# Score products of two sub-heads issued in turn, for a whole tile at once

## The chip, the cores and the metric

One NeuronCore of a Trainium2 chip runs the whole kernel. The metric is the device time of one execution in microseconds (us). Before the change the median of three runs is 1964.11 us (1963.23 to 1964.5).

## What is computed

The program is one layer of a streaming encoder for two groups of tokens, 1024 prompt tokens and 64 sample tokens, that share all weights: a modulated norm, two token mixers side by side (HGRN2 with 4 heads of 128 key channels, GLA with 4 heads of 64 key channels), a gated merge and an output projection, then a routed mixture of 32 experts and a final norm. All data is fp32. The change lies in the GLA mixer, of which this is the core, for chunks of 64 tokens:

```python
b = cumsum(log_a)                                   # per key channel
o_inter = (q * exp(b)) @ S
diff = b[t] - b[s]
decay = exp(where(causal, diff, 0)) * causal
scores[t, s] = sum_k q[t, k] * k[s, k] * decay[t, s, k]
o = o_inter + scores @ v
S = exp(b_last) * S + (k * exp(b_last - b)).T @ v
```

The decay depends on the key channel, so the scores are no single matrix product. The kernel splits the causal triangle of a chunk into levels of halves (64, 32, ..., 1 tokens). For each level the decay splits into a factor of the key's token and one of the query's token, so that a level is one product of two prepared arrays, of which a mask keeps the blocks that belong to this level.

## The kernel before

The kernel is a row of stages; in each, every engine has its own instruction list, written out by hand, and waits on semaphores. There is no planner. The stage `mixers` runs over six units: two GLA units of two heads each (sub-heads, 64 key channels each, on the lower and the upper 64 partitions), then four HGRN2 units of one head with 128 channels. `SUB[u]` is 2 or 1. A unit projects its inputs for all tokens (matmuls of 360 or 364 tokens, lines 128 to 130), prepares the levels, and then runs a loop over tiles: eight of 128 tokens and one of 64. A step `j` of the loop is one sub-head of one tile, `i, sub = divmod(j, SUB[u])`; a GLA unit has 18 steps.

In a step TensorE does, in this order:

- `turn` (lines 528, 530), at the last sub-head of a tile: transposes the keys and values of the next tile into `p_tok`.
- `scores(u, j + 1)` (lines 544, 547): for each of 7 levels and each half of 64 tokens one product of 64 by 64, from the partitions of the sub-head, into `p_sc[:, j % 2]`, and for a tile of 128 tokens one more product for the cross block (keys of the first half, queries of the second). An fp32 matmul is two instructions. Token half 0 writes output partitions 0 to 63, half 1 writes 64 to 127; each `p_sc[:, x]` is 512 fp32 columns wide, a bank of its own. Before it, `scores(u, j)` waits until all masks up to `j - 2` are through (`sc_masked`) and the cross copies up to there (`cross_ready`).
- the filling: projections of the next unit or gates still to be made (`filled(u, j)`). In a GLA unit nine column blocks are spread over 18 steps, one in each even step.
- `outputs(u, j)` (lines 568 to 570): the old state with the queries, the scores `sc[:, j % 2]` with the values, and the update of the state into `p_u`.

VectorE does in step `j`: `mask(u, j + 1)`, then `advance(u, j)` (line 1010, the state, only at the last sub-head of a tile, after both `outputs`), then other work of the step: the low half of the next weights (`next_low`, line 1022, the step after a filling with a new block), `gate_g` at step 3, `gate_g_scale` at 5, `decay_log` (line 899) three steps and `decay_bound` four steps after the next unit's first block is filled (steps 7 and 8), `gate_x` of the third gate at 13. Within `mask` (lines 990, 995, 997) the order is:

```python
dve.wait_ge(sc_done, after(J0[u] + j + 1))
V.tensor_tensor(diag[...j % 2], p_sc[...j % 2, 0:NL * 64], masks, ALU.mult)   # sc_masked
dve.wait_ge(o_done, after(J0[u] + j - 1))          # outputs up to j - 2 done
V.tensor_copy(sc[0:64, j % 2, 64:P], p_sc[...])    # cross_ready
V.tensor_reduce(...)  # one per half of 64 tokens, sc_ready
```

ScalarE keeps the outputs (`keep_output`), the turned tiles (`keep_tok`, line 747), the projections (`keep`) and computes the exponentials of gates and decays.

Of the kernel before, what the change touches and what calls it, by code (L numbers as in the profile page):

```python
# [34 lines left out]
P = 128  # L35
# [5 lines left out]
NT = T_PROMPT // P  # L41
TILES = [(i * P, P) for i in range(NT)] + [(T_PROMPT, T_SAMPLE)]
# [10 lines left out]
NL = len(HALVES)  # L53
# [3 lines left out]
def after(n):  # L57

    return n + START
# [311 lines left out]
def mixers(nc, a, h_hi, h_lo, ident, mix_d, gate_d, outs, consts):  # L371
# [5 lines left out]
    SUB = [2 if kind == "gla" else 1 for kind, _ in UNITS]  # L377
    NS = [(NT + 1) * n for n in SUB]
# [36 lines left out]
    def filled(u, j):  # L415

        groups = filling(u)
        now = groups[-(-len(groups) * j // NS[u]):-(-len(groups) * (j + 1) // NS[u])]
        return [g for some in now for g in some]
# [14 lines left out]
    with Stage(nc, "x") as s:  # L434
# [69 lines left out]
        @block.tensor  # L504
        def _(pe):
            def project(u, name, c):

                c0, n = COLS[c]
                e = place[(u, name), c]
                pe.wait_ge(proj_kept, after(e - 1))  # L510
                if name == "logit":
                    i = UNITS[u][1]
                    nc.tensor.matmul(p_proj[:, e % 2, 0:n], gk2[:, i * P:(i + 1) * P], lr[:, c0:c0 + n],
                                     start=True, stop=True).then_inc(proj_done, 1)
                    return
                i = load_no[u, name]
                if c == 0:
                    pe.wait_ge(w_lo_done, after(i + 1))
                for k_ in range(KD):
                    m = split_matmul(nc, p_proj[:, e % 2, 0:n], (w_hi[:, i % 2, k_, :], w_lo[:, i % 2, k_, :]),  # L520
                                     (h_hi[:, k_, c0:c0 + n], h_lo[:, k_, c0:c0 + n]), k_ == 0, k_ == KD - 1)
                m.then_inc(proj_done, 1)

            def turn(u, i):

                t0, n = TILES[i]
                pe.wait_ge(tok_kept, after(u * (NT + 1) + i))
                nc.tensor.transpose(p_tok[0:n, 0:P], ke[:, t0:t0 + n], ident[:, :])
                for sub in range(SUB[u]):
                    m = nc.tensor.transpose(p_tok[0:n, (1 + sub) * P:(2 + sub) * P], v[sub][:, t0:t0 + n], ident[:, :])  # L530
                m.then_inc(tok_turned, 1)

            def scores(u, j):

                i, sub = divmod(j, SUB[u])
                t0, n = TILES[i]
                ch = slice(sub * (P // SUB[u]), (sub + 1) * (P // SUB[u]))
                pe.wait_ge(sc_masked, after(J0[u] + j - 1))
                pe.wait_ge(cross_ready, after(X0[u] + min(j, NT * SUB[u]) - 1))
                for l in range(NL):  # L540
                    for h0 in range(0, n, 64):
                        tt = slice(t0 + h0, t0 + h0 + 64)
                        left, right = (k[u % 2], q) if l == 0 else (lev[:, l], lev[:, l])
                        m = nc.tensor.matmul(p_sc[h0:h0 + 64, j % 2, l * 64:(l + 1) * 64], left[ch, tt], right[ch, tt],
                                             start=True, stop=True)
                if n == P:
                    m = nc.tensor.matmul(p_sc[0:64, j % 2, NL * 64:NL * 64 + 64], lev[ch, 0, t0:t0 + 64],  # L547
                                         lev[ch, 0, t0 + 64:t0 + P], start=True, stop=True)
                m.then_inc(sc_done, 1)

            def outputs(u, j):

                i, sub = divmod(j, SUB[u])
                t0, n = TILES[i]
                ch = slice(sub * (P // SUB[u]), (sub + 1) * (P // SUB[u]))
                po = p_o[:, j % 2, 0:n]
                vt = tok[:, i % 2, 1 + sub, :]
                if sub == 0:
                    pe.wait_ge(tok_kept, after(u * (NT + 1) + i + 1))
                    if i == 0:  # L560
                        pe.wait_ge(state_zero, after(u + 1))
                    if i == NT:
                        pe.wait_ge(state_in, landed(u + 1))
                    pe.wait_ge(state_ready, after(u * (NT + 1) + i))
                pe.wait_ge(o_kept, after(J0[u] + j - 1))
                pe.wait_ge(sc_ready, after(J0[u] + j + 1))
                pe.wait_ge(cross_ready, after(X0[u] + min(j + 1, NT * SUB[u])))
                nc.tensor.matmul(po, state[ch, i % 2 if i < NT else 2, :], qe[ch, t0:t0 + n], start=True, stop=False)
                nc.tensor.matmul(po, vt[:, :], sc[:, j % 2, 0:n], start=False, stop=True).then_inc(o_done, 1)
                nc.tensor.matmul(p_u[ch, 0:DV], tok[0:n, i % 2, 0, ch], vt[0:n, :], start=True, stop=True).then_inc(u_done, 1)  # L570

            def mean_square(u, sub, c):

                c0, n = COLS[c]
                pe.wait_ge(o_sq, after(H0[u] + sub + 1))
                pe.wait_ge(rstd_ln, after((H0[u] + sub) * NC + c))
                nc.tensor.matmul(p_tok[:, 0:n], mean[:, :], t1[:, c0:c0 + n], start=True, stop=True).then_inc(ms_done, 1)

            pe.wait_ge(lr_split, after(2))
            for c, (c0, n) in enumerate(COLS):  # L580
                if c:
                    pe.wait_ge(lr_kept, after(c))
                for k_ in range(KD):
                    m = split_matmul(nc, p_tok[0:RANK, 0:n], (lr_hi[:, k_, :], lr_lo[:, k_, :]),
                                     (h_hi[:, k_, c0:c0 + n], h_lo[:, k_, c0:c0 + n]), k_ == 0, k_ == KD - 1)
                m.then_inc(lr_done, 1)
            pe.wait_ge(lr_kept, after(NC))
            for name in first(0):
                for c in range(NC):
                    project(0, name, c)  # L590
            for u in range(NU):
                for n_, name in enumerate(middle(u)):
                    for c in range(NC):
                        project(u, name, c)
                        if u and n_ == 0 and c > 0:
                            mean_square(u - 1, 0, c - 1)
                        if u and n_ == 1 and c == 0:
                            mean_square(u - 1, 0, 2)
                        if u and n_ == 2 and SUB[u - 1] == 2:
                            mean_square(u - 1, 1, c)  # L600
                pe.wait_ge(lev_ready, after((u + 1) * NL))
                pe.wait_ge(ends_ready, after(2 * u + 2))
                pe.wait_ge(proj_kept, kept(u, f"v{SUB[u] - 1}"))
                pe.wait_ge(rstd_ln, after(H0[u] * NC))
                turn(u, 0)
                scores(u, 0)
                for j in range(NS[u]):
                    if j + 1 < NS[u]:
                        if (j + 1) % SUB[u] == 0:
                            turn(u, (j + 1) // SUB[u])  # L610
                        scores(u, j + 1)
                    for (of, name), c in filled(u, j):
                        project(of, name, c)
                    outputs(u, j)
            for c in range(NC):
                mean_square(NU - 1, 0, c)

        @block.scalar
        def _(act):
# [167 lines left out]
            for u in range(NU):  # L787
# [72 lines left out]
                for j in range(NS[u]):  # L860
                    if j:
                        keep_output(u, j - 1)
                    if j + 1 < NS[u] and (j + 1) % SUB[u] == 0:
                        keep_tok(u, (j + 1) // SUB[u])
                    for (of, name), c in filled(u, j):
                        keep(of, name, c)
                    if j < 3:
                        gate_g_part(u, SUB[u] - 1, j)
                    if j == 4:
                        gate_g_exp(u, SUB[u] - 1)  # L870
                    if u + 1 < NU and 0 <= j - filled_by(u, first(u + 1)[0]) < 3:
                        decay_part(u + 1, j - filled_by(u, first(u + 1)[0]))
                    if not HG[u]:
                        if 0 <= j - filled_by(u, "x2") < 3:
                            gate_x_part(u, 2, j - filled_by(u, "x2"))
                        if j == filled_by(u, "x2") + 4:
                            gate_x_out(u, 2)
# [1350 lines left out]
```

## Time and profile before

| | |
|---|---|
| median of 3 runs | 1964.11 us |
| the profiled execution | 1957.79 us |
| its span, first to last instruction | 1955.9 us |
| mean granted TensorE clock | 0.915 |
| TensorE busy | 1624.9 us (83%) |
| VectorE busy | 1285.5 us (66%) |
| ScalarE busy | 956.5 us (49%) |
| score products, line 544 (PE), GLA tiles | 816 + 136 instructions, 218 to 271 ns each |

### The profile page before, as it was taken

The page shows a single profiled execution, that of the slowest core. Times are in us where ns is not written, and L with a number is a line of the kernel's source. Part 1 is how long each engine was busy: PE and PEld are TensorE (multiplying, and loading weights), DVE is VectorE, ACT ScalarE, POOL GpSimd, SP SyncE. Part 2 cuts the span into 40 slices and gives each one's busy share as a digit, 9 for nine tenths or more (in the row PEclk, how much of TensorE's full clock was granted, in tenths as well). Part 3 has the DMA queues.
Part 4 walks back from the last instruction along what each step waited for, and adds up shares of the span by engine and source line. Part 5 has one row for each costly group of instructions (what it writes and reads, how often), then busy time and mean ns, then how long its engine had stood idle before and what let it go on. Part 6 is the DMA issues. An engine that isn't in the chain of part 4 may idle for free. (4 is left out here: it accounts for less than half of the span.)

```text
span 1955.9 us, 26699 instructions
## 1 busy us (share of the span) xinstructions
PE 1624.9 (83%) x10674; PEld 1414.9 (72%) x10674; DVE 1285.5 (66%) x1623; ACT 956.5 (49%) x1182; POOL 322.2 (16%) x187
## 2 busy tenths in 40 slices
PE   3679999999798999983896995089999999999810
PEld 2459989988698998983895774078888888888710
DVE  2534368267658585854554656189999999999727
ACT  2624335333525353533102211178888888888713
POOL 0110001000101010101220000512232233233113
PEclk8789999999999999996898897589999999999955
DMA  8822102201111111104325322689999999999546
GB/s 323 293 54 69 35 12 70 81 21 34 64 51 49 47 47 57 36 37 169 121 96 186 121 91 63 167 309 370 377 378 380 383 376 370 377 381 382 217 166 236
DMA packets 193154, 347.01 MB, mean 177 GB/s; under 512 B 22514, under 2 KB 78282, under 8 KB 191948
## 3 DMA queue, kind: packets, MB, share of 16 engines
q1 hardware_dynamic: 175644, 308.43, 44.7%
q10 hardware_dynamic: 7536, 19.08, 2.5%
q0 software_dynamic: 9856, 17.86, 2.4%
q8 instruction: 83, 1.36, 0.3%
q14 instruction: 35, 0.29, 0.0%
HBM read 316.66 MB, written 44.38 MB: 185 GB/s over the span
## 5 line engine op out<-in xcount | busy, mean ns | idle before, releaser
L128 PE MATMUL x_psum_proj<-h_hi,x_w_hi 128*128 128x364 f32 (+1 forms) x1056 | 362.6, 343 | 23.8 <-ACT x_v L643 11.8
L129 PE MATMUL x_psum_proj<-h_lo,x_w_hi 128*128 128x364 f32 (+1 forms) x1056 | 351.0, 332 | 0.0
L130 PE MATMUL x_psum_proj<-h_hi,x_w_lo 128*128 128x364 f32 (+1 forms) x1056 | 350.8, 332 | 0.0
L128 PEld LDWEIGHTS x_psum_proj<-h_hi,x_w_hi 128*128 128x128 f32 x1056 | 202.1, 191 | 32.8 <-ACT x_v L643 12.7
L129 PEld LDWEIGHTS x_psum_proj<-h_lo,x_w_hi 128*128 128x128 f32 x1056 | 202.3, 192 | 2.5 <-issue 0.3
L130 PEld LDWEIGHTS x_psum_proj<-h_hi,x_w_lo 128*128 128x128 f32 x1056 | 201.9, 191 | 0.0
L502 POOL CAST x_w_hi<-x_w 128x1024 fp32r<-128x1024 f32 x44 | 73.5, 1670 | 663.8 <-PE x_psum_proj L130 662.0
L1712 POOL DMA_INDIRECT scratch_y<-e_y,e_tbl x32 | 87.9, 2748 | 414.7 <-ACT e_y L1765 414.7
L1794 DVE TENSOR_TENSOR e_g_lo<-ew_w,e_g_hi 128x2048 fp32r<-128x2048 f32 x64 | 143.8, 2289 | 11.5 <-ACT e_g_hi L1740 11.5
L1794 DVE TENSOR_TENSOR e_d_lo<-ew_w,e_d_hi 128x2048 fp32r<-128x2048 f32 x64 | 143.4, 2281 | 1.1 <-ACT e_d_hi L1740 1.1
L1794 DVE TENSOR_TENSOR e_u_lo<-ew_w,e_u_hi 128x2048 fp32r<-128x2048 f32 x64 | 143.5, 2283 | 0.6 <-ACT e_u_hi L1740 0.6
L997 DVE TENSOR_REDUCE x_sc<-x_diag 64x64 f32<-64x448 f32 x136 | 127.1, 935 | 1.1
L1740 ACT ACTIVATE e_d_hi<-ew_w 128x2048 fp32r<-128x2048 f32 x64 | 119.2, 1922 | 0.0
L1740 ACT ACTIVATE e_g_hi<-ew_w 128x2048 fp32r<-128x2048 f32 x64 | 118.5, 1901 | 0.0
L1740 ACT ACTIVATE e_u_hi<-ew_w 128x2048 fp32r<-128x2048 f32 x64 | 118.5, 1902 | 0.0
L128 PE MATMUL e_psum_g<-e_g_hi,e_x_hi 128*128 128x512 f32 x256 | 105.2, 411 | 11.9 <-DVE e_x_lo L1799 10.1
L990 DVE TENSOR_TENSOR x_diag<-x_psum_sc,all_shapes 128x448 f32<-128x448 f32 (+1 forms) x72 | 44.6, 619 | 97.7 <-PE x_psum_sc L547 93.8
L1022 DVE TENSOR_TENSOR x_w_lo<-x_w,x_w_hi 128x1024 fp32r<-128x1024 f32 x44 | 53.6, 1220 | 83.0 <-POOL x_w_hi L502 82.9
L128 PE MATMUL e_psum_y<-e_d_hi,e_hid_hi 128*128 128x512 f32 x256 | 103.1, 403 | 5.4 <-DVE e_d_lo L1794 5.4
L129 PE MATMUL e_psum_g<-e_g_lo,e_x_hi 128*128 128x512 f32 x256 | 101.5, 397 | 0.0
L130 PE MATMUL e_psum_g<-e_g_hi,e_x_lo 128*128 128x512 f32 x256 | 100.9, 394 | 0.0
L130 PE MATMUL e_psum_y<-e_d_hi,e_hid_lo 128*128 128x512 f32 x256 | 100.3, 392 | 0.0
(294 smaller groups left out, 3606.8 us busy)
## 6 DMA issues: line engine op xcount, KB each, us to landing
ew_w<-in_w_e_gate SPq DMA_DIRECT2D x64, 1024.0 KB, 10.6
ew_w<-in_w_e_up SPq DMA_DIRECT2D x64, 1024.0 KB, 8.1
ew_w<-in_w_e_down SPq DMA_DIRECT2D x64, 1024.0 KB, 9.2
c_w<-in_w_ada SPq DMA_DIRECT2D x12, 2048.0 KB, 16.6
x_w<-in_w_in SPq DMA_DIRECT2D x44, 512.0 KB
scratch_gate<-x_x ACTq DMA_DIRECT2D x16, 544.0 KB, 2.7
m_gate<-scratch_gate SPq DMA_DIRECT2D x16, 544.0 KB, 4.5
z_y<-scratch_y SPq DMA_DIRECT2D x8, 1024.0 KB, 7.5
```

The lines of the kernel that those rows point to most:

```text
L128: nc.tensor.matmul(out, lhs[0], rhs[0], start=start, stop=False)
L129: nc.tensor.matmul(out, lhs[0], rhs[1], start=False, stop=False)
L130: return nc.tensor.matmul(out, lhs[1], rhs[0], start=False, stop=stop)
L502: nc.gpsimd.tensor_copy(w_hi[:, n % 2], w[:, n % 2]).then_inc(w_hi_done, 1)
L990: V.tensor_tensor(diag[0:n, j % 2], p_sc[0:n, j % 2, 0:NL * 64].rearrange("p (l t) -> p l t", t=64), masks[0:n], ALU.mult).then_inc(sc_mas ...
L997: red = V.tensor_reduce(sc[h0:h0 + 64, j % 2, h0:h0 + 64], diag[h0:h0 + 64, j % 2].rearrange("p l t -> p t l"), AX.X, ALU.add)
L1022: V.tensor_tensor(w_lo[:, n % 2], w[:, n % 2], w_hi[:, n % 2].bitcast(F32), ALU.subtract).then_inc(w_lo_done, 1)
L1712: nc.gpsimd.indirect_dma_start(out=y_d, out_offset=bass.IndirectOffsetOnAxis(ap=tbl[:, e:e + 1], axis=0), in_=y[:, e % 2, :], in_offset=No ...
L1740: nc.scalar.activation(his[part][:, half_rows(part, half), :], staged(part, e, half), ACT.Copy).then_inc(hi_done[part], 1)
L1794: V.tensor_tensor(los[part][:, rows, :], staged(part, e, half), his[part][:, rows, :].bitcast(F32), ALU.subtract).then_inc(lo_done[part], 1)
```

## The change

TensorE gets `scores_pair(u, i)`, which does the scores of both sub-heads of tile `i`: for each level and each half of 64 tokens first sub-head 0, then sub-head 1, then the two cross products. It waits until all masks and cross copies of the tile before are through. The GLA units call it for tile 0 ahead of the loop, and at each even step `j` for tile `j // 2 + 1`, right after the `turn` of that tile, ahead of the step's filling and of both `outputs` of tile `j // 2`. The `turn` moves with it, from the odd step before. On ScalarE `keep_tok` moves to the same even step. HGRN2 units keep the order they had.

```diff
--- before.py
+++ after.py
@@ -548,6 +548,28 @@
                                          lev[ch, 0, t0 + 64:t0 + P], start=True, stop=True)
                 m.then_inc(sc_done, 1)
 
+            def scores_pair(u, i):
+
+                t0, n = TILES[i]
+                j = 2 * i
+                pe.wait_ge(sc_masked, after(J0[u] + j))
+                pe.wait_ge(cross_ready, after(X0[u] + min(j, NT * 2)))
+                for l in range(NL):
+                    for h0 in range(0, n, 64):
+                        tt = slice(t0 + h0, t0 + h0 + 64)
+                        left, right = (k[u % 2], q) if l == 0 else (lev[:, l], lev[:, l])
+                        for sub in range(2):
+                            ch = slice(64 * sub, 64 * sub + 64)
+                            m = nc.tensor.matmul(p_sc[h0:h0 + 64, sub, l * 64:(l + 1) * 64], left[ch, tt], right[ch, tt],
+                                                 start=True, stop=True)
+                            if n < P and l == NL - 1:
+                                m.then_inc(sc_done, 1)
+                if n == P:
+                    for sub in range(2):
+                        ch = slice(64 * sub, 64 * sub + 64)
+                        nc.tensor.matmul(p_sc[0:64, sub, NL * 64:NL * 64 + 64], lev[ch, 0, t0:t0 + 64],
+                                         lev[ch, 0, t0 + 64:t0 + P], start=True, stop=True).then_inc(sc_done, 1)
+
             def outputs(u, j):
 
                 i, sub = divmod(j, SUB[u])
@@ -603,12 +625,17 @@
                 pe.wait_ge(proj_kept, kept(u, f"v{SUB[u] - 1}"))
                 pe.wait_ge(rstd_ln, after(H0[u] * NC))
                 turn(u, 0)
-                scores(u, 0)
+                if HG[u]:
+                    scores(u, 0)
+                else:
+                    scores_pair(u, 0)
                 for j in range(NS[u]):
-                    if j + 1 < NS[u]:
-                        if (j + 1) % SUB[u] == 0:
-                            turn(u, (j + 1) // SUB[u])
+                    if HG[u] and j + 1 < NS[u]:
+                        turn(u, j + 1)
                         scores(u, j + 1)
+                    if not HG[u] and j % 2 == 0 and j + 2 < NS[u]:
+                        turn(u, j // 2 + 1)
+                        scores_pair(u, j // 2 + 1)
                     for (of, name), c in filled(u, j):
                         project(of, name, c)
                     outputs(u, j)
@@ -860,8 +887,8 @@
                 for j in range(NS[u]):
                     if j:
                         keep_output(u, j - 1)
-                    if j + 1 < NS[u] and (j + 1) % SUB[u] == 0:
-                        keep_tok(u, (j + 1) // SUB[u])
+                    if j % SUB[u] == 0 and j + SUB[u] < NS[u]:
+                        keep_tok(u, j // SUB[u] + 1)
                     for (of, name), c in filled(u, j):
                         keep(of, name, c)
                     if j < 3:
```

## Rows read from the trace of the kernel before

**Rows 1.** Stretch, length, then busy us of PE, PEld, DVE, ACT, POOL; then granted clock.

```profile
225.00:310.00 85.00, 85.00 (x870) 71.47 (x869) 56.33 (x86) 25.53 (x51) 4.17 (x4) 1.00 0.09 27
399.00:476.00 77.00, 77.00 (x832) 66.01 (x833) 57.13 (x85) 22.69 (x45) 2.88 (x3) 1.00 0.10 30
```

**Rows 2.** TensorE in time, one tile: start, length, engine, line.

```profile
261.73 0.48 PE L568 MATMUL x_psum_o<-x_qe,x_state 64*128 64x128 f32 x2
262.14 0.49 PE L569 MATMUL x_psum_o<-x_sc,x_tok 128*128 128x128 f32 x2
...
263.40 0.33 PE L544 MATMUL x_psum_sc<-x_q,x_k 64*64 64x64 f32 x4
...
264.48 0.48 PE L568 MATMUL x_psum_o<-x_qe,x_state 64*128 64x128 f32 x2
...
266.74 0.43 PE L128 MATMUL x_psum_proj<-h_hi,x_w_hi 128*128 128x364 f32 x1
...
270.93 0.37 PE L568 MATMUL x_psum_o<-x_qe,x_state 64*128 64x128 f32 x1
```

**Rows 3.** TensorE at the start of the first GLA unit.

```profile
225.69 0.33 PE L544 MATMUL x_psum_sc<-x_q,x_k 64*64 64x64 f32 x4
...
226.45 0.27 PE L544 MATMUL x_psum_sc<-x_q,x_k 64*64 64x64 f32 x1
...
226.56 0.22 PE L547 MATMUL x_psum_sc<-x_lev 64*64 64x64 f32 x1
226.56 0.22 PE L544 MATMUL x_psum_sc<-x_q,x_k 64*64 64x64 f32 x1
...
227.52 0.43 PE L128 MATMUL x_psum_proj<-h_hi,x_w_hi 128*128 128x364 f32 x1
```

**Rows 4.** TensorE at the last tile of that unit.

```profile
298.54 0.48 PE L568 MATMUL x_psum_o<-x_qe,x_state 64*128 64x128 f32 x2
...
303.29 0.43 PE L128 MATMUL x_psum_proj<-h_hi,x_w_hi 128*128 128x360 f32 x1
```

**Rows 5.** VectorE in time, one tile of the first GLA unit.

```profile
274.44 0.22 DVE L995 COPY x_sc<-x_psum_sc 64x64 f32<-64x64 f32 x1
...
276.45 0.35 DVE L1010 SCALAR_TENSOR_TENSOR x_state<-x_state,x_eb_last,x_psum_u 128x128 f32<-128x128 f32 x1
...
277.37 0.22 DVE L995 COPY x_sc<-x_psum_sc 64x64 f32<-64x64 f32 x1
```

**Rows 6.** VectorE, and TensorE's load that waited for it, last unit.

```profile
868.99 0.35 DVE L1010 SCALAR_TENSOR_TENSOR x_state<-x_state,x_eb_last,x_psum_u 128x128 f32<-128x128 f32 x1
...
869.41 0.30 PEld L568 LDWEIGHTS x_psum_o<-x_qe,x_state 128*128 128x128 f32 x2 [1.15 <-issue]
```

**Rows 7.** VectorE, other work of a step.

```profile
267.53 1.22 DVE L1022 TENSOR_TENSOR x_w_lo<-x_w,x_w_hi 128x1024 fp32r<-128x1024 f32 x1
268.67 1.28 DVE L899 SCALAR_TENSOR_TENSOR x_t<-x_b,x_t 128x1088 f32<-128x1088 f32 x1
```

**Rows 8.** VectorE, second mask's copy of the unit.

```profile
230.26 0.22 DVE L995 COPY x_sc<-x_psum_sc 64x64 f32<-64x64 f32 x1
```

**Rows 9.** TensorE after a gap in time, and granted clock by stretch.

```profile
508.09 0.43 PE L128 MATMUL x_psum_proj<-h_hi,x_w_hi 128*128 128x364 f32 x1 [1.57 <-ACT x_x L643]
...
508.10:511.00 2.90, 2.90 (x17) 2.90 (x18) 2.87 (x4) 0.30 (x1) 0.47 (x1) 1.00 0.64 181
...
634.58 0.67 PE L128 MATMUL x_psum_proj<-h_hi,x_w_hi 128*128 128x360 f32 x1 [3.93 <-ACT x_v L643]
...
635.35 0.50 PE L130 MATMUL x_psum_proj<-h_hi,x_w_lo 128*128 128x360 f32 x1
...
639.55 0.34 PE L129 MATMUL x_psum_proj<-h_lo,x_w_hi 128*128 128x360 f32 x1
...
897.25 1.55 PE L577 MATMUL x_psum_tok<-x_t,all_mean 128*128 128x364 f32 x2 [2.95 <-ACT x_t L759]
...
895.60:899.00 3.40, 1.55 (x2) 0.50 (x2) 1.29 (x1) 1.67 (x3) 0.00 (x0) 0.50 0.00 0
```

## Prediction, made before the changed kernel was run

> **What bounds the kernel now.** I read the busy time by stretch first, then the time-ordered lists of TensorE and VectorE inside it. The change touches only the two GLA units of the mixer stage. In their token loops TensorE is busy for all of the time, 85.00 of 85.00 us and 77.00 of 77.00, at full granted clock [rows 1]; nobody makes it wait there, while VectorE has about a third of the stretch free. So, before the change, time taken off TensorE in these loops is time off the kernel, and a wait put into them is time added.
>
> One tile of 128 tokens is two sub-heads, and TensorE's order is: outputs(2i), turn, scores, outputs(2i+1), scores, filling projection. The rows give it [rows 2], from the start of outputs(2i) at 261.73: turn ended and scores begin at 263.40 (1.67 later), one scores call takes 1.08 (263.40 to 264.48), the filling begins at 266.74, so the whole is 5.01 and one outputs call 5.01 - 1.67 - 2 x 1.08 = 1.18. The filling takes 4.19 (266.74 to 270.93).
>
> **What the pair costs TensorE.** A scores call of one sub-head is 15 products, 30 instructions, in 1.08 us. By the code seven levels and the cross block make 8 x 2 = 16 places of about 0.06 us each (1.08 / 16, start and end included) if the products for tokens 0 to 63 and 64 to 127 run side by side, in two halves of the array's columns. Whether the other sub-head (other half of the rows) runs beside them is shown at one place: at a unit's start scores(0) and scores(1) follow each other, and the q,k products of sub-head 1 start at 226.45, before the cross product of sub-head 0 at 226.56 [rows 3]. From 225.69 to the filling at 227.52 both calls take 1.83, not 2 x 1.08 = 2.16. So four products share a place where the order lets them, and I take 1.09 for a pair call (one call and two more starts). The other end is 2.16, two calls with nothing shared.
>
> By the Trainium skill, "TensorE: Matmul & The Clock Gate", section "Back-to-back issue gap", matmuls never start less than about 25 ns apart, however small; four to a place would then need 100 ns instead of about 60, an estimate from that page of some 0.6 us more a pair and 12 us in all. The rows speak against it for different parts of the array: a cross product of sub-head 0 and a q,k product of sub-head 1 both start at 226.56 [rows 3].
>
> If nothing else changed, a unit would give: at each of 7 tile boundaries 5.01 - (1.67 + 1.18 + 1.09) = 1.07; at the last tile, where [rows 4] show 4.75 from outputs(14) to the filling and two outputs calls alone need 2.4, 2.35; at the start two pairs and a turn (1.09 + 0.49 + 1.09 = 2.67, the turn being 1.67 - 1.18) instead of 1.83, a loss of 0.84. That is 9.0 a unit, 18 us for two.
>
> **What the pair has to wait for.** scores_pair(i+1) overwrites both banks of p_sc, so it waits for the masks and cross copies of both sub-heads of tile i (all masks up to 2i+1). Before, a scores call needed only the mask two calls back, which is why no wait shows. And the pair now stands ahead of the filling and of outputs(2i), outputs(2i+1) of the tile before, while mask(j)'s copy and reduction write sc[j % 2], still read by outputs(j-2). VectorE works in the order mask(2i+2), advance(2i+1), other work of the step, mask(2i+3), and only after mask(2i+3)'s copy may scores_pair(i+2) start. Mask(2i+2) gets its scores before the filling, but its copy must wait for outputs(2i), which comes after the filling. The filling hides none of this chain.
>
> The chain, counted from the start of outputs(2i):
> - o_done at 0.90 (262.14 + 0.49 - 261.73 [rows 2]), hand-off 0.04: copy starts at 0.94.
> - Copy and two reductions, to the start of advance: 2.01 (274.44 to 276.45 [rows 5]): 2.95. Advance needs outputs(2i+1), over by 1.18 + 1.3 = 2.5, so it does not wait.
> - Advance and the masking product up to the next copy: 0.92 (276.45 to 277.37), copy 0.22 [rows 5]: 4.09. Its own wait, outputs(2i+1), is over.
> - Hand-off VectorE to TensorE 0.07 (868.99 + 0.35 to 869.41 [rows 6]): the pair starts at 4.16, where TensorE was ready at 1.18 + 1.67 = 2.85.
>
> So the stall is 1.31, and a boundary costs 4.16 + 1.09 = 5.25 against 5.01: +0.24, seven times, +1.7 a unit. The gain of 1.07 is eaten by the bare chain.
>
> Then the other work. What VectorE does at an odd step, after advance and before mask(2i+3), was beside the filling; now it stands in the chain. By the code these are the weight halves at steps 1, 7 and 13 (1.14 each, 267.53 to 268.67 [rows 7]), gate_g at 3, gate_g_scale at 5, decay_log at 7 and gate_x(2) at 13 (1.20 each: 1.28 at 268.67, less the overlap of 0.08 that the row before it shows, 1.22 long and 1.14 to the next [rows 7]). Sum 3 x 1.14 + 4 x 1.20 = 8.2 a unit. Decay_bound is at step 8, even, beside the filling: nothing. Their own inputs come from ScalarE before the filling ends or just behind it; nothing is added for them.
>
> At a unit's start scores_pair(1) is issued right behind scores_pair(0) and must wait for mask(0), its reductions, mask(1) and its copy. Before, that copy ended at 230.26 + 0.22 = 230.48 [rows 8], 4.79 after the scores began at 225.69; the pair starts at 4.86 and the filling at 5.95, against 1.83: +4.12. The last tile keeps its gain of 2.35, and 0.1 is gained as the sample tile's pair is shorter.
>
> Sum for a unit: 4.1 + 1.7 + 8.2 - 2.4 - 0.1 = +11.5; for two +23 us. The ends of the unknown in it: with a pair at 2.16 it is 1.07 x 9 x 2 = 19 more; below, 0, as the pair holds a whole call for either half of the rows and so takes no less than the 1.08 of one. ScalarE's keep_tok, moved from odd to even steps, waits for the turn that also moved, and the buffer it fills was last read a tile ago: 0, with outputs(2i) four us behind as cover, and 0.49 a tile if that cover were gone. Transitions between units follow the last outputs as before, as VectorE and ScalarE both have to wait for these.
>
> **The clock.** TensorE never idled here; now it idles, end to start, 0.1 less than the stall: about 3.2 at a unit's start, 1.2 at two boundaries, 2.4 at three (after steps 1, 3, 5) and 3.6 at two (7, 13). Such gaps elsewhere [rows 9]: after 1.57 the clock stayed 1.00; after 2.95 it was 0.50 (1.2 instead of 2.4 GHz); after 3.93 a projection matmul takes 0.50 instead of 0.34 and full pace returns at 639.55, 5.0 later. At half clock the stream needs nearly twice the time: 3.4 us of it lose 1.6, those 5.0 some 2.3. The three gaps over 2.95 in a unit I price at 1.6 each, 9.6 for two units; the 2.4 ones lie between the row that kept the clock and the one that lost it, half of them at 1.6: 4.8. Part of the low clock falls into idle time, so I take 12 for 14.4. The ends are 0 and 6 x 2.3 + 6 x 1.6 = 23.
>
> **Sum.** 23 + 12 = +35 us. The profiled execution took 1957.79 us around its span of 1955.9, the median of the runs is 1964.11, 0.3% more; a difference carries over: 1964.1 + 35 = 1999.
>
> **Rivals.**
> - The chain as above, but the clock keeps its level through gaps of about three us: 1964 + 23 = 1987. For it: only one or two rows show the fall. Against: 2.95 was enough there.
> - TensorE isn't held: VectorE is through in time, and the saved scores calls come out in full, -18: 1946. It would need the chain of 4.16 to fit into 2.85, so 1.3 us shorter and without the step's other work; that is the point from which it decides. For it: VectorE is idle a third of the loop and gets no more work. Against: the order of waits in mask(), which I find no way around.
> - Products of the two sub-heads don't share the array, as the order within a level (same columns, different rows) is one that [rows 3] show only for a short stretch: pair 2.16 and +19 on top, 2018 with the clock cost, less if shared in part (2007 to 2015). The page's 25 ns would land here too.
>
> **How the numbers follow.** Forecast 0.72, clock rival 0.12, no sharing or half of it 0.10, TensorE not held 0.06. The range runs from a little under the clock rival, 1985, to half the no-sharing cost and a worse clock, 2013; below it is the fast rival, above it the full no-sharing. A change of this kernel under 0.2% (4 us) can't be told from none. Faster 0.05, same 0.02 (chain and gain about cancelling), slower 0.93.
>
> **What would show it.** Right: in the GLA loops TensorE idle before the q,k score products, released by VectorE's copy, 1.2 us at the plain boundaries and 2.4 or 3.6 where the step has other work, 3.2 at the start of a unit; the first GLA loop 11 to 18 us longer than its 84; lower clock in slices that had full; a pair call of about 1.1. Wrong: no idle time there, or the loops shorter; a pair call near 2.2 would move the cause to the array; gaps with the clock at 1.00 throughout, the clock term.

## Result: the changed kernel is slower, 2010.3 us against 1963.7

| | before | changed |
|---|---|---|
| median of 4 runs | 1963.67 us | 2010.3 us (2008.67 to 2015.17) |
| ratio, 95% interval | | 1.0256 (1.0236 to 1.0275) |
| profiled execution, span | 1957.79, 1955.9 us | 2008.67, 2006.8 us |
| first GLA loop, first scores to last outputs | 82.8 us | 105.3 us |
| second GLA loop | 80.4 us | 107.3 us |

The ratio is an estimate of its own, with its interval, and isn't the quotient of the two medians in the table. By the medians the change costs 46.6 us, by the ratio 50 (46 to 54), and the profiled execution is 50.9 us longer. Medians below come with their ratio to runs of the kernel before, whose median was between 1959.9 and 1963.7 us from one set of runs to the next.

Of the 50.9 us, 49.3 lie in the two GLA loops; an HGRN2 loop takes 43.4 us in both. (Before the change the last outputs of the second GLA loop start at 479.3 and not at the 476 named above.) The page of the changed kernel, with what answers to the slices before:

```profile
span 2006.8 us, 26681 instructions
...
PE 1630.5 (81%) x10674; PEld 1421.8 (71%) x10674; DVE 1287.6 (64%) x1623; ACT 956.3 (48%) x1182; POOL 321.9 (16%) x187
...
PE   3579878988979898988497898069999999999910
...
PEclk8789989997989999999698899579999999999955
```

The same two loops by busy time, columns as in [rows 1], show that TensorE is no longer busy throughout and that its granted clock is no longer 1.00 (it is 0.89 and 0.83). Below them stands the list of whom TensorE waits for in these loops (us in total, times, longest):

```profile
226.47:331.70 105.23, 84.13 (x857) 71.13 (x856) 55.71 (x84) 25.00 (x50) 3.85 (x4) 0.89 0.07 22
422.10:529.40 107.30, 86.19 (x852) 74.56 (x851) 56.85 (x85) 23.37 (x47) 3.94 (x4) 0.83 0.07 22
```

```profile
PE x_psum_sc L563 <- DVE x_sc L1022: 42.2, 16, 3.7
```

Where [rows 2] show no wait, all sixteen pair calls inside the loops now wait for VectorE's cross copy, 42.2 us in total. VectorE's busy time in the loops is what it was; only its place against TensorE has changed.

A plain boundary is one between two tiles at which VectorE has no other work of the step. One of them, TensorE in time, which answers to [rows 2]:

```profile
290.21 0.48 PE L590 MATMUL x_psum_o<-x_qe,x_state 64*128 64x128 f32 x2
290.62 0.49 PE L591 MATMUL x_psum_o<-x_sc,x_tok 128*128 128x128 f32 x2
...
291.40 0.48 PE L590 MATMUL x_psum_o<-x_qe,x_state 64*128 64x128 f32 x2
...
292.60 0.33 PE L528 MATMUL x_psum_tok<-all_ident,x_ke 128*128 128x128 f32 x1
292.76 0.38 PE L530 MATMUL x_psum_tok<-all_ident,x_v 128*128 128x128 f32 x2
294.51 0.34 PE L563 MATMUL x_psum_sc<-x_q,x_k 64*64 64x64 f32 x8 [1.36 <-DVE x_sc L1022]
294.64 0.91 PE L563 MATMUL x_psum_sc<-x_lev 64*64 64x64 f32 x48
...
299.78 0.48 PE L590 MATMUL x_psum_o<-x_qe,x_state 64*128 64x128 f32 x2
```

and VectorE beside it, which answers to [rows 5]:

```profile
291.22 0.22 DVE L1022 COPY x_sc<-x_psum_sc 64x64 f32<-64x64 f32 x1 [4.86 <-PE x_psum_o L591]
291.36 1.84 DVE L1024 TENSOR_REDUCE x_sc<-x_diag 64x64 f32<-64x448 f32 x2
293.23 0.35 DVE L1037 SCALAR_TENSOR_TENSOR x_state<-x_state,x_eb_last,x_psum_u 128x128 f32<-128x128 f32 x1
293.50 0.62 DVE L1017 TENSOR_TENSOR x_diag<-x_psum_sc,all_shapes 128x448 f32<-128x448 f32 x1
294.15 0.22 DVE L1022 COPY x_sc<-x_psum_sc 64x64 f32<-64x64 f32 x1
```

The chain can be read off line by line: outputs(2i) ends its L591 product at 291.11, the waiting copy starts at 291.22, reductions, advance (L1037), the next masking product and the next copy follow without a hole until 294.37, and the pair starts at 294.51. That is 4.30 us after 290.21; the turn had ended 1.36 us before.

The next boundary is the same, but here the clock falls behind the gap. The 48 level products take 1.53 us instead of 0.91 and the projection matmuls 0.67 and 0.48 until 0.33 is back at 307.75:

```profile
304.11 0.49 PE L563 MATMUL x_psum_sc<-x_q,x_k 64*64 64x64 f32 x8 [1.39 <-DVE x_sc L1022]
304.35 1.53 PE L563 MATMUL x_psum_sc<-x_lev 64*64 64x64 f32 x48
...
306.01 0.67 PE L128 MATMUL x_psum_proj<-h_hi,x_w_hi 128*128 128x364 f32 x1
...
307.09 0.48 PE L128 MATMUL x_psum_proj<-h_hi,x_w_hi 128*128 128x364 f32 x1
...
307.75 0.33 PE L128 MATMUL x_psum_proj<-h_hi,x_w_hi 128*128 128x364 f32 x1
```

### The profile page after: what moved, and what is told of

Read it like the earlier page. It is cut to its first block and busy times, and to the rows that moved or that the text cites. A ratio compares the mean times of both kernels' runs of the same rounds, so it can differ in the third digit from the quotient of the medians.

```text
span 2006.8 us, 26681 instructions
## 1 busy us (share of the span) xinstructions
PE 1630.5 (81%) x10674; PEld 1421.8 (71%) x10674; DVE 1287.6 (64%) x1623; ACT 956.3 (48%) x1182; POOL 321.9 (16%) x187
## 3 DMA queue, kind: packets, MB, share of 16 engines
q1 hardware_dynamic: 175644, 308.43, 43.4%
q8 instruction: 83, 1.36, 0.3%
## 5 line engine op out<-in xcount | busy, mean ns | idle before, releaser
L128 PE MATMUL x_psum_proj<-h_hi,x_w_hi 128*128 128x364 f32 (+1 forms) x1056 | 371.4, 352 | 23.8 <-ACT x_v L670 11.8
L129 PE MATMUL x_psum_proj<-h_lo,x_w_hi 128*128 128x364 f32 (+1 forms) x1056 | 358.4, 339 | 0.0
L130 PE MATMUL x_psum_proj<-h_hi,x_w_lo 128*128 128x364 f32 (+1 forms) x1056 | 357.4, 338 | 0.0
L128 PEld LDWEIGHTS x_psum_proj<-h_hi,x_w_hi 128*128 128x128 f32 x1056 | 208.5, 197 | 33.8 <-ACT x_v L670 12.7
L129 PEld LDWEIGHTS x_psum_proj<-h_lo,x_w_hi 128*128 128x128 f32 x1056 | 208.9, 198 | 2.4 <-issue 0.2
L130 PEld LDWEIGHTS x_psum_proj<-h_hi,x_w_lo 128*128 128x128 f32 x1056 | 208.1, 197 | 0.0
L670 ACT ACTIVATE x_x<-x_psum_proj 128x364 f32<-128x364 f32 (+1 forms) x48 | 22.1, 469 | 166.8 <-PE x_psum_proj L130 166.8
L129 PE MATMUL e_psum_y<-e_d_lo,e_hid_hi 128*128 128x512 f32 x256 | 100.5, 393 | 0.0
```

The lines of the kernel that those rows point to most:

```text
L128: nc.tensor.matmul(out, lhs[0], rhs[0], start=start, stop=False)
L129: nc.tensor.matmul(out, lhs[0], rhs[1], start=False, stop=False)
L130: return nc.tensor.matmul(out, lhs[1], rhs[0], start=False, stop=stop)
L670: nc.scalar.activation(dst[:, c0:c0 + n], p_proj[:, e % 2, 0:n], ACT.Copy).then_inc(proj_kept, 1)
```

## Experiments

All are the changed kernel with one edit or two. How long the clock was low is worked out from the mean granted clock of a loop: 0.89 over 105.2 us is 23 us at half. A loop is counted from its first scores to its last outputs.

| kernel | median us | ratio to before | loops us | clock in them |
|---|---|---|---|---|
| changed | 2010.3 | 1.0256 | 105.3, 107.3 | 0.89, 0.83 |
| clock_kept | 1986.3 | 1.0123 | 96.4, 93.1 | 0.98, 1.00 |
| short_gaps_left | 1990.0 | 1.0138 | 96.8, 93.0 | 0.98, 1.00 |
| pair_in_a_row | 2038.3 | 1.0394 | 119.4, 117.7 | 0.81, 0.80 |
| in_a_row_clock_kept | 2002.1 | 1.0199 | 102.1, 98.7 | 0.98, 1.00 |
| other_work_later | 1984.8 | 1.0129 | 92.1, 93.1 | 0.94, 0.91 |
| four_score_buffers | 1994.6 | 1.0169 | 101.3, 97.8 | 0.88, 0.90 |
| masks_first | 1951.2 | 0.9953 | 76.0, 76.0 | 1.00, 0.98 |
| filling_first_in_a_row | 1953.9 | 0.9967 | 78.7, 76.3 | 1.00, 1.00 |
| filling_first | 1937.2 | 0.9876 | 72.1, 69.6 | 1.00, 1.00 |

### Is it the clock? Gaps filled with products

```diff
+            def warm(u, j):
+                (of, name), c = filled(u, j)[0]
+                e, i, (c0, n) = place[(of, name), c], load_no[of, name], COLS[c]
...
+                for _ in range((17, 13, 13, 13, 20, 5, 5, 20)[j // 2]):
+                    nc.tensor.matmul(p_proj[:, e % 2, 0:n], w_hi[:, i % 2, 0, :], h_hi[:, 0, c0:c0 + n], start=True, stop=True)
             def scores_pair(u, i):
...
+                warm(u, j - 2)
                 pe.wait_ge(sc_masked, after(J0[u] + j))
```

> The changed kernel, with projection products repeated on TensorE ahead of each wait of a pair call (17, 13, 13, 13, 20, 5, 5 and 20 of them, about 0.2 us less than each gap), into the bank that the step's filling overwrites later. Theory (the waiting chain plus the clock that the gaps take down): the chain stays as long as it is, the clock stays at 1.00 in both GLA loops, and the 24 us that I read as low clock go: about 1986 us (1981 to 1991), loops of 95.5 and 93 us from the first scores to the last outputs. Rival (what the loops lost beyond the chain is not the clock but something in the pair calls and fillings themselves): 2006 to 2012 us, clock at 1.00 or not.

Measured 1986.3 us, 1.0123 (1.0102 to 1.0144): 24 us less by giving TensorE more to do. The windows of both loops and the waits in them:

```profile
225.85:322.30 96.45, 93.19 (x964) 79.94 (x963) 56.05 (x84) 25.03 (x50) 3.92 (x4) 0.98 0.08 24
412.60:505.70 93.10, 89.42 (x958) 77.61 (x956) 57.24 (x85) 23.43 (x47) 3.93 (x4) 1.00 0.08 25
```

```profile
PE x_psum_sc L575 <- DVE x_sc L1034: 6.9, 15, 0.6
```

The pairs start as late as in the changed kernel, 4.30 us after outputs(2i) at a plain boundary (the chain is VectorE's), and the leftover gaps of 0.4 to 0.6 add to 6.9 us. With the clock up the loops are 13.6 and 12.7 us longer than before the change, which is the chain alone. So of the 49.3 us that the loops lost, 26 are the chain and 23 are the clock: about half each. The result lies inside the expectation, and the rival, 2006 us or more, is out.

The clock did fall once in the first loop, and no gap stood near: the last one before it, of 0.39 us, ended at 242.37.

```profile
243.00:250.80 7.80, 7.80 (x71) 6.17 (x61) 2.99 (x6) 2.45 (x5) 0.00 (x0) 1.00 0.21 62
250.90:254.20 3.30, 3.30 (x13) 3.30 (x14) 3.23 (x6) 0.49 (x1) 0.00 (x0) 0.50 0.00 0
```

> clock_kept with fewer repeated products (12, 7, 7, 7, 15, 0, 0, 15), so that all 16 gaps stay at about 1.4 us and the chain stays the same. Theory: gaps of 1.4 us that come once every nine us bring the clock down at some boundaries and not at others, as the two plain boundaries of a unit and other_work_later showed: some 10 us of low clock over clock_kept, 1996 us (1989 to 2003), the longest of all repeats different by several us. Rival (a gap has to reach 2.5 us, as the kernel before kept its clock through 1.57): 1984 to 1988 us.

Its edit is the same with the counts (12, 7, 7, 7, 15, 0, 0, 15). Measured 1990.0 us, 1.0138 (1.0114 to 1.0162), at the low end of the theory's range and 2 us above the rival's. Of sixteen gaps of 1.2 to 1.45 us in the profile, one was followed by the low clock, and the profiled loops are as long as those of clock_kept (189.8 and 189.5 us in sum). That a short gap lowers the clock now and then stands, at a much lower rate than I expected; that it costs time isn't shown, as the intervals of the two kernels overlap.

### What the interleaving is worth

```diff
-                for l in range(NL):
...
-                        for sub in range(2):
+                for sub in range(2):
+                    ch = slice(64 * sub, 64 * sub + 64)
+                    for l in range(NL):
```

> The changed kernel with the pair call in the same place and behind the same waits, but all products of sub-head 0 and then all of sub-head 1. Theory: the two calls share the array only where they meet, as at the start of a unit before the change (1.83 us for two against 1.09), and the call is part of the chain, so each of 18 calls costs 0.75 us more: about 2024 us (2018 to 2030). Rival (the order within the call is worth nothing, since TensorE waits anyway): 2007 to 2013 us. If four products at once were slower than two, below 2007.

Measured 2038.3 us, 1.0394 (1.0363 to 1.0426): 28 more than the changed kernel, where 14 were expected, and above the range. To part order and clock, the same with the gaps filled (the first count is 13 in place of 17):

> pair_in_a_row (2038 us) with the gaps filled as in clock_kept (1986 us). It tells what of the 28 us between pair_in_a_row and the changed kernel is the order in the call and what is the clock. Theory: a call in a row takes 1.83 instead of 1.09; the first call of a unit is hidden behind the masks, the eight others are in the chain: 6 us a unit, 12 in all over clock_kept, 1998 us (1993 to 2003), and the other 16 of the 28 were low clock. Rival (products in a row cost 28 by themselves): 2010 us or more.

Measured 2002.1 us, 1.0199 (1.0173 to 1.0225). Its loops are 5.7 and 5.6 us longer than those of clock_kept; that is the eight calls of a unit at 0.7 each, as expected, and the first call is hidden behind the masks. The other 4 of the 16 us between the two medians lie outside the loops. pair_in_a_row's loops are 36 us longer than these: its clock was at half for 45 and 47 us of them (0.81 and 0.80). The changed kernel's are 23 longer than clock_kept's, so 13 of the 28 us are additional low clock, where 16 were expected.

### What stands in the chain

other_work_later moves VectorE's other work behind the next mask:

```diff
+                    late = 0 if HG[u] else 1
-                    for (of, name), c in filled(u, j - 1) if j else []:
+                    for (of, name), c in filled(u, j - 1 - late) if j > late else []:
...
-                    if j == 3:
+                    if j == 3 + late:
                         gate_g(u, SUB[u] - 1)
```

> The changed kernel with VectorE's other work of the GLA steps (weight halves, gate_g, gate_g_scale, decay_log, decay_bound, gate_x) done one step later, behind the mask that TensorE waits for. Theory: 8.2 us a unit leave the chain, 16 in all, each boundary has the plain gap of 1.4, and with the long gaps part of the low clock goes too (half of the 14 short gaps and both at the start at 1.5 to 1.8, 13 instead of 24): about 1983 us (1975 to 1992). Rival (that work was hidden or is waited for elsewhere, so moving it gives nothing): 2007 to 2013 us.

Measured 1984.8 us, 1.0129 (1.0106 to 1.0153). All gaps but those at a unit's start (3.21) and two more (2.00 and 3.19) are 1.36 to 1.40 now. Four of the twelve short ones were followed by the low clock, where half were expected, and all three over 3 us. The expectation holds in its time. The two longer gaps come from the edit itself: one step later decay_bound stands at step 9, which is odd, so between advance and the next masking product (0.64 us at 284.20 in the first loop, 1.83 at 464.15 in the second).

four_score_buffers gives the reduced scores four buffers (`sc` of 4, `j % 4`, `o_done` up to `j - 3`):

> The changed kernel with four buffers for the reduced scores in place of two, so that the copy and reductions of mask(2i+2) need not wait for outputs(2i) and run beside the filling; mask(2i+3) still stands behind advance(2i+1) and the other work. Theory: the chain then starts at the end of outputs(2i+1), 2.5 us from the start of outputs(2i), and the pair starts at 3.7 in place of 4.3 at a plain boundary, so 0.5 to 0.6 less at each of 14 boundaries, 8 us, and 2 to 6 of low clock: 36 us over the kernel before in place of 47 (30 to 41), plain gaps 0.8 to 0.9 us. Rival (the wait on outputs(2i) is the whole cause): all gaps but those at a unit's start gone, under 1960 us. Rival (that wait holds nothing): gaps of 1.36 us as they are.

Measured 1994.6 us, 1.0169 (1.014 to 1.0198), 35 over the kernel before where 36 were expected. At a plain boundary advance is now the first in the chain, and the gap is 0.84:

```profile
291.92 0.35 DVE L1037 SCALAR_TENSOR_TENSOR x_state<-x_state,x_eb_last,x_psum_u 128x128 f32<-128x128 f32 x1 [5.27 <-PE x_psum_u L592]
292.19 0.62 DVE L1017 TENSOR_TENSOR x_diag<-x_psum_sc,all_shapes 128x448 f32<-128x448 f32 x1
292.84 0.21 DVE L1022 COPY x_sc<-x_psum_sc 64x64 f32<-64x64 f32 x1
```

```profile
293.20 0.34 PE L563 MATMUL x_psum_sc<-x_q,x_k 64*64 64x64 f32 x8 [0.84 <-DVE x_sc L1022]
```

So the wait on outputs(2i) is one link, worth 0.5 us a boundary, and taking it alone does not free TensorE. What is left is the place of mask(2i+3) in VectorE's list, behind advance and the other work.

masks_first changes VectorE's order in the GLA loops, at odd steps:

```diff
-                    if j + 1 < NS[u]:
-                        mask(u, j + 1)
-                    advance(u, j)
...
+                    elif j % 2 == 1:
+                        if j + 1 < NS[u]:
+                            mask_a(u, j + 1)
+                            mask_a(u, j + 2)
+                        advance(u, j)
+                        if j + 1 < NS[u]:
+                            mask_b(u, j + 1)
+                            mask_b(u, j + 2)
```

`mask_a` is the masking product and the cross copy, `mask_b` the reductions. As `diag` has two buffers, `mask_a` also waits for the reductions of two masks before (`sc_ready`).

> The changed kernel, pair call in its place, two score buffers, but VectorE does masking product and cross copy of both sub-heads first, then advance, then the reductions of both and the other work. Theory: the reductions (1.85 us), advance (0.3) and the other work were in the chain only by their place in VectorE's list; without them the copy of mask(2i+3) ends 2.4 us after the start of outputs(2i), and TensorE is ready at 2.85: no gap at the boundaries, one of about 1.3 us at each unit's start in place of 3.2, full clock. About 1945 us (1938 to 1952). Rival (reductions done later keep outputs waiting, or the copies need something else): gaps move ahead of outputs and the time stays over 1960 us.

Measured 1951.2 us, 0.9953 (0.9936 to 0.997): the pair in its place, two buffers, and faster than before the change. The waits:

```profile
PE x_psum_sc L563 <- DVE x_sc L1027: 5.4, 4, 1.7
```

Four waits are left: 1.7 and 1.4 us at the starts, about the 1.3 expected, and 0.6 and 1.7 at the boundary behind step 7 of each unit, which I had not expected. There the weight half, decay_log and decay_bound stand behind 3.9 us of reductions and make VectorE late for the next masks. These two waits and a spell of low clock in the second loop (0.98, 1.5 us lost) account for 4 of the 6 us between 1951 and 1945; the time is inside the expected range.

### The filling ahead of the pair

```diff
                     if not HG[u] and j % 2 == 0 and j + 2 < NS[u]:
                         turn(u, j // 2 + 1)
-                        scores_pair(u, j // 2 + 1)
                     for (of, name), c in filled(u, j):
                         project(of, name, c)
+                    if not HG[u] and j % 2 == 0 and j + 2 < NS[u]:
+                        scores_pair(u, j // 2 + 1)
                     outputs(u, j)
```

> The changed kernel with the filling of an even step put between turn and scores_pair, so that VectorE has 4.2 us more before the pair needs its copies. Theory: the chain (4.3 us and up to 2.3 of other work, from the start of outputs(2i)) fits into the 7.0 that TensorE now has to do before the pair, all gaps go, and the saved scores calls come out in full: about 1946 us (1943 to 1950), no idle time of TensorE in the loops. Rival (outputs right behind the pair now wait for the reductions of their masks, a new gap of one to two us a tile): 1960 to 1990 us.

Measured 1937.2 us, 0.9876 (0.9856 to 0.9896), the fastest of all, 23 us under the kernel before by the medians and 24 by the ratio. That is below the expected range, which ended at 1943; its mechanism (no wait of TensorE left in the loops) holds. TensorE in its loops, and one tile of it:

```profile
225.90:298.00 72.10, 72.10 (x858) 60.93 (x857) 56.07 (x84) 26.00 (x50) 3.92 (x4) 1.00 0.11 32
388.40:458.00 69.60, 69.60 (x851) 60.05 (x850) 57.41 (x85) 24.26 (x47) 3.84 (x4) 1.00 0.11 33
```

```profile
250.85 0.48 PE L590 MATMUL x_psum_o<-x_qe,x_state 64*128 64x128 f32 x2
...
252.05 0.49 PE L590 MATMUL x_psum_o<-x_qe,x_state 64*128 64x128 f32 x2
...
253.25 0.33 PE L528 MATMUL x_psum_tok<-all_ident,x_ke 128*128 128x128 f32 x1
...
253.55 0.41 PE L128 MATMUL x_psum_proj<-h_hi,x_w_hi 128*128 128x364 f32 x1
...
257.72 0.34 PE L563 MATMUL x_psum_sc<-x_q,x_k 64*64 64x64 f32 x8
...
258.59 0.28 PE L570 MATMUL x_psum_sc<-x_lev 64*64 64x64 f32 x4
258.80 0.48 PE L590 MATMUL x_psum_o<-x_qe,x_state 64*128 64x128 f32 x2
```

The turn (253.25) is followed by the filling and this by the pair (257.72), with no wait. A tile takes 7.95 us from outputs to outputs (250.85 to 258.80), where [rows 2] have 9.20. It gives 1.25 a tile against 1.07 worked out. The pair call (1.08) and the filling (253.55 to 257.72, 4.17) are as forecast; the turn is what got shorter. It takes 0.30 (253.25 to 253.55) with projections behind it, where before the change it took 0.47 with the 64 by 64 score products behind it (to 263.40 in [rows 2], from this row):

```profile
262.93 0.33 PE L528 MATMUL x_psum_tok<-all_ident,x_ke 128*128 128x128 f32 x1
```

That a change of the shape of the products costs this 0.17 is my reading; no run varies it alone.

> The filling put ahead of scores_pair, as in filling_first (1937 us), with all products of sub-head 0 and then all of sub-head 1 in the call. Where TensorE never waits, the order inside the call is the only difference. Theory: the interleaved order is worth the overlap of the sub-heads, 1.83 us less 1.09 in 18 calls: 13 us more than filling_first, about 1951 us (1947 to 1955), and still some 9 us below the kernel before, since a pair call in one piece saves changes between kinds of matmuls (each tile has two fewer). Rival A (the order is worth nothing, the place of the call is all): 1935 to 1941 us. Rival B (the order is worth the whole gain): 1957 to 1964 us.

Measured 1953.9 us, 0.9967 (0.9952 to 0.9982). The loops are 6.6 and 6.7 us longer than those of filling_first, so the order is worth 13 us, as expected. (The medians lie 17 us apart; the other 4 are outside the loops.) The loops are still 4.1 us each under those of the kernel before, which is what one call at this place saves over two calls without the interleaving.

## Why the prediction was wrong

The direction, the place and the mechanism were right: VectorE's chain from outputs(2i) over both masks' copies holds the pair. The size was not: +35 us was forecast, and +46.6 measured by the medians, +50 by the ratio. The median of 2010.3 is near the high end of the range, 2013; the ratio laid on 1964.1 gives 2014. The GLA loops became 22.5 and 26.9 us longer, where the first was said to become 11 to 18 longer.

- **The chain.** It was forecast at 4.16 at a plain boundary and measured 4.30 (294.51 - 290.21). The gaps were forecast at 3.2, 2.4, 2.4, 2.4, 3.6, 1.2, 1.2, 3.6 and measured at 3.21, 2.53, 2.58, 2.60, 3.71, 1.36, 1.39, 3.73. That is about 0.14 more at each but the first, as the hand-offs around the copy took longer (291.11 to 291.22, 294.37 to 294.51) than 0.04 and 0.07. The sum is +25 for two units in place of 23, and clock_kept bears it out with 26.3 in its loops.
- **The pair call.** 1.09 was forecast; 226.47 to 227.55 is 1.08 at a unit's start, 60 instructions at 18 ns each, the rows that end this section. Four products share the array, and filling_first_in_a_row prices that at 13 us. The price for no sharing counted nine calls a unit; in_a_row_clock_kept shows eight, as the first is hidden behind the masks. By the Trainium skill, "TensorE: Matmul & The Clock Gate", section "Back-to-back issue gap", matmuls start no closer than about 25 ns; the trace disagrees for products in different parts of the array, and the measurement decides.
- **The clock is the step that failed.** It was "so I take 12 for 14.4", and the measured cost is 24, above even the high end of 23 that was given for it. From the start of a pair to the next outputs the stream takes 5.27 us at full clock (294.51 to 299.78; 6.07 where a logit product ends the filling, 5.13 at the last tile). The changed kernel takes 1.4 to 2.8 us more than that behind 13 of its 16 gaps, 10 us in the first loop and 14 in the second, so 1.85 each. By the kinds of gap that the prediction had:

| gaps in two units | lowered the clock, said | measured | cost, said | measured |
|---|---|---|---|---|
| six of 3.2 or 3.6 us | 6 | 6 | 9.6 us | 10 us |
| six of 2.4 us | 3 | 5 | 4.8 us | 11 us |
| four of 1.2 us | 0 | 2 | 0 | 3 us |
| less what falls into idle time | | | 2.4 us | in the rows above |

So half of the error of 12 sits in the 2.4 us gaps: more of them lowered the clock, and behind three of those (and behind one of the long gaps) it stayed low long enough to cost 2.3 to 2.8. Two of the short gaps lowered it too, although [rows 9] had a gap of 1.57 that did not. In all the clock was at half for some 60 us of the two loops. [rows 9] had shown no gap between 1.57 and 2.95, so the half for the 2.4 ones had no row behind it, and I took the five slow microseconds behind the gap of 3.93 for the high side of the range only. Filling the gaps gave 24 us back. Three pair calls of the first loop up to the next outputs, with gaps of 2.53, 2.58 and 2.60 before them, columns as in [rows 1]:

```profile
244.35:251.95 7.60, 7.59 (x86) 6.80 (x86) 2.27 (x3) 0.47 (x1) 0.00 (x0) 0.78 0.25 71
257.47:265.98 8.51, 8.51 (x86) 7.66 (x86) 2.24 (x3) 0.47 (x1) 0.59 (x1) 0.67 0.00 0
271.52:276.79 5.27, 5.27 (x85) 4.97 (x85) 2.27 (x3) 0.00 (x0) 0.00 (x0) 1.00 0.02 3
```

- **Rivals.** "The clock keeps its level" would have been 1987: that is what clock_kept measures, with the clock held by hand. "TensorE isn't held" fell with the first wait; its price of -18 lies between what lifting the waits gives: -23 in filling_first and -9 in masks_first, which keeps four of them. "No sharing" fell with the 1.08.
- **Where the gain of the change went.** It is there, as filling_first shows. Against that kernel the loops of the changed one are 71 us longer, of which 42 are waits and 24 low clock. The pair was put where it frees nothing, as VectorE had its slack beside the filling and the pair stands in front of it.

The first pair call of the changed kernel, TensorE in time, up to the turn behind it (8 + 48 + 4 instructions):

```profile
226.47 0.34 PE L563 MATMUL x_psum_sc<-x_q,x_k 64*64 64x64 f32 x8
226.64 0.88 PE L563 MATMUL x_psum_sc<-x_lev 64*64 64x64 f32 x48
227.34 0.28 PE L570 MATMUL x_psum_sc<-x_lev 64*64 64x64 f32 x4
227.55 0.33 PE L528 MATMUL x_psum_tok<-all_ident,x_ke 128*128 128x128 f32 x1
```

## What to carry to other kernels

Joining two calls halves their buffering: a call that overwrites both buffers waits for everything that reads either. Before putting it somewhere, list for the engine that reads them all that stands in its program between the two reads. Then put the longest independent work of the writing engine between (filling_first), or let the reading engine do first what the writer waits for (masks_first). Price a new gap on TensorE with the clock that follows it, which here cost 24 us beside 42 us of waits.

## What the runs showed of the hardware that was not expected

- Gaps of the same length may or may not lower TensorE's clock: 1.36 us before 294.51 did not, 1.39 before 304.11 did. The gaps in front of the pair calls, in the profiles of six kernels (changed, short_gaps_left, pair_in_a_row, other_work_later, four_score_buffers, masks_first):

| gap, us | followed by the low clock |
|---|---|
| 3.17 to 3.73 | 19 of 19 |
| 2.47 to 2.60 | 13 of 14 |
| 1.97 to 2.04 | 4 of 7 |
| 1.24 to 1.45 | 11 of 37: 2 of 4 changed, 1 of 16 short_gaps_left, 4 of 12 other_work_later, 4 of 4 pair_in_a_row, 0 of 1 masks_first |
| 0.56 to 0.84 | 0 of 5 |

The two gaps left out, 1.70 (low clock behind it) and 1.74 (none), are both of masks_first. The length isn't all: at 1.24 to 1.45 the share differs from kernel to kernel, and in clock_kept the clock fell once in a stretch without a gap. What decides it stays open.
- Four fp32 products of 64 by 64 in the four quarters of the array run in the time of two: 1.08 us for 30 products, where one sub-head's 15 took 1.08.
